# Attention steps: the transposes of the probabilities in turn with projection matmuls on TensorE

## The reference

```python
h = _rms_norm(x, norm_attn_g[l])
proj = h @ w_in[l]
qa, ka, va, fa, qb, kb, vb, ga, gb = jnp.split(proj, split_points, axis=-1)
log_f = jax.nn.log_sigmoid(fa.astype(jnp.float32) + b_forget[l].astype(jnp.float32))
oa = _fox_attention(qa..., ka..., va..., log_f)      # 8 heads of 64, causal, with a forget bias
qb = _partial_rope(qb..., positions)
kb = _partial_rope(kb..., positions)
ob = _dilated_mixture(qb, kb, vb...)                 # 12 heads of 64, windows with dilation 1, 4, 16
ya = oa.reshape(B, S, FOX_W) @ w_branch_a[l]
yb = ob.reshape(B, S, DIL_OUT_W) @ w_branch_b[l]
mixed = jax.nn.sigmoid(ga) * ya + jax.nn.sigmoid(gb) * yb
x = x + mixed @ w_out[l]
h = _rms_norm(x, norm_mlp_g[l])
x = x + jnp.square(jax.nn.relu(h @ w_up[l])) @ w_down[l]
```

## Time and profile before

| what | before |
| --- | --- |
| median of three runs | 1581.77 us |
| lowest and highest run | 1577.9 and 1582.29 us |
| the profiled execution's own time | 1580.75 us |
| its span, first to last instruction | 1578.9 us |
| TensorE matmul busy | 1508.9 us (96%), 7364 instructions |
| VectorE busy | 1094.0 us (69%) |
| ScalarE busy | 797.1 us (50%) |
| mean granted TensorE clock | 0.993 |

### The profile page before, as it was taken

The page is one execution under the profiler, slowest core; times in us unless marked ns, Lnnn a source line. Parts: engine busy times, 40 slices in busy tenths (PEclk is TensorE's granted clock), DMA queues, the critical chain, the costliest instruction groups (busy, mean ns, idle before and its releaser), DMA issues. The chain is left out here.

```text
span 1578.9 us, 20832 instructions
## 1 busy us (share of the span) xinstructions
PE 1508.9 (96%) x7364; PEld 1242.5 (79%) x7364; DVE 1094.0 (69%) x1747; ACT 797.1 (50%) x1438; POOL 9.5 (1%) x24
## 2 busy tenths in 40 slices
PE   6999999998999999999999999999999899999997
PEld 5788887886888888788888878888888677777776
DVE  5687777755756768843665676666666887777776
ACT  5577666653767775534224453343334444444442
POOL 1000000000000000000000000000000000000001
PEclk9999999999999999999999999999999999999999
DMA  5321111111022113333635424444446664444402
GB/s 187 95 67 28 41 54 41 31 38 27 19 63 68 28 41 91 97 107 107 214 120 160 134 86 150 165 151 149 147 147 210 236 226 147 147 147 147 147 27 107
DMA packets 168277, 173.40 MB, mean 110 GB/s; under 512 B 7848, under 2 KB 127720, under 8 KB 167792
## 3 DMA queue, kind: packets, MB, share of 16 engines
q1 hardware_dynamic: 168176, 172.07, 33.9%
HBM read 125.84 MB, written 46.20 MB: 109 GB/s over the span
## 5 line engine op out<-in xcount | busy, mean ns | idle before, releaser
L1131 PE MATMUL ps<-hspl,wsp 128*128 128x512 f32 x1536 | 422.5, 408 | 6.6 <-ACT tmp L1572 3.1
L1131 PEld LDWEIGHTS ps<-hspl,wsp 128*128 128x128 f32 x1536 | 265.0, 189 | 53.1 <-ACT tmp L1572 5.8
L1483 PE MATMUL ps<-dn_b,a_hi 128*128 128x512 f32 x896 | 280.1, 394 | 18.7 <-DVE keep L2328 13.1
L1483 PEld LDWEIGHTS ps<-dn_b,a_hi 128*128 128x128 f32 x896 | 168.2, 190 | 61.1 <-issue 22.9
L1483 PE MATMUL ps<-dn_b,a_lo 128*128 128x512 f32 x448 | 175.8, 392 | 0.0
L2328 DVE TENSOR_TENSOR keep<-keep,ps 128x512 f32<-128x512 f32 (+1 forms) x144 | 101.6, 713 | 41.7 <-PE ps L1483 23.4
L1483 PE MATMUL ps<-up_b,a_hi 128*128 128x512 f32 x384 | 118.5, 390 | 0.6 <-DVE up_b L2328 0.6
L1944 ACT ACTIVATE keep<-keep 128x512 f32<-128x512 f32 x64 | 40.5, 633 | 125.6 <-DVE keep L2630 42.0
L1483 PEld LDWEIGHTS ps<-dn_b,a_lo 128*128 128x128 f32 x448 | 84.8, 189 | 17.9
L2328 DVE TENSOR_TENSOR dn_b<-dn_raw,dn_b 128x1024 fp32r<-128x1024 f32 x56 | 67.1, 1221 | 39.4 <-ACT dn_b L1960 39.4
L2215 DVE TENSOR_TENSOR keep<-ps,o_part 64x256 f32<-64x256 f32 x80 | 39.7, 496 | 76.8 <-ACT o_part L1665 76.3
(11 more groups left out here) (242 smaller groups left out, 2823.9 us busy)
## 6 DMA issues: line engine op xcount, KB each, us to landing
hidden<-keep SPq DMA_DIRECT2D x112, 256.0 KB, 2.2
dn_raw<-hidden SPq DMA_DIRECT2D x56, 512.0 KB, 6.1
raw<-in_w_in SPq DMA_DIRECT2D x35, 512.0 KB, 3.7
a_raw<-in_w_up SPq DMA_DIRECT2D x36, 256.0 KB, 3.1
sgl<-sg SPq DMA_DIRECT2D x8, 1024.0 KB, 5.1
a_raw<-in_w_down SPq DMA_DIRECT2D x32, 256.0 KB, 3.1
spare<-in_w_down SPq DMA_DIRECT2D x32, 256.0 KB, 3.9
spare<-in_w_up SPq DMA_DIRECT2D x28, 256.0 KB, 3.2
```

The lines of the kernel that those rows point to most:

```text
L1131: ins = pe.matmul(psp(u, g), wsp[c % 2][:, wp, k * P:(k + 1) * P], hspl[:, mp, k, cols], start=(n == 0), stop=(n == 23), skip_group_check= ...
L1483: ins = pe.matmul(o, a_part(n, j, wp, k), b_block(n, j, mp, k), start=(first and k == 0 and m == 0), stop=(k == ks - 1 and m == 2), skip_g ...
```

## The change: what it does, and the diff

On TensorE, `project_part` goes, and two helpers take its place. `share(G)` gives what group a step works on, how many matmuls are the step's and which part of the group. `project_next(G, a, b)` issues the step's matmuls from a to b. `transposes` now takes how many of the next step's matmuls are issued already (`ahead`) and whether there is a step to take them from (`more`); behind each transpose it issues one projection matmul while the step has any left, and it gives the new count back. In `mixer_steps` the first third stays ahead of the transposes, and what is left of the step's matmuls after them follows. A step's set of instructions, the waits and the signals are the same.

```diff
-            def project_part(G, part):
+            def share(G):
                 t, s = divmod(G, STEPS)
-                if t < MIX:
-                    for u, g, steps in group_steps(t):
-                        if s in steps:
-                            per = 24 // len(steps)
-                            a = (s - steps[0]) * per
-                            project(u, g, a + per * part // 3, a + per * (part + 1) // 3)
+                return [(u, g, 24 // len(steps), s - steps[0]) for u, g, steps in group_steps(t) if s in steps]
+
+            def project_next(G, a, b):
+
+                for u, g, per, n in share(G):
+                    if a < min(b, per):
+                        project(u, g, n * per + a, n * per + min(b, per))
...
-            def transposes(G):
+            def transposes(G, ahead, more):
+
                 pe.wait_ge(exp_done, G + 1)
...
                     for k in range(a, b):
                         ins = pe.transpose(PS[2][:, (u % 2) * HALF + (k - a) * P:(u % 2) * HALF + (k - a + 1) * P],
                                            probs(G)[:, k * P:(k + 1) * P], ident[:])
-                    ins.then_inc(tr_done, 1)
+                        if k == b - 1:
+                            ins.then_inc(tr_done, 1)
+                        if more:
+                            project_next(G + 1, ahead, ahead + 1)
+                            ahead += 1
+                return ahead
...
+                    ahead = sum(per // 3 for _, _, per, _ in share(G)) if G < last else 0
                     if G < last:
-                        project_part(G, 0)
+                        project_next(G, 0, ahead)
                     if first <= G - 1 < last:
-                        transposes(G - 1)
+                        ahead = transposes(G - 1, ahead, G < last)
                     if G < last:
-                        project_part(G, 1)
-                    if G < last:
-                        project_part(G, 2)
+                        project_next(G, ahead, 24)
```

## The result

The changed kernel takes 1589.74 us (median of seven runs, 1587.31 to 1593.36) against 1582.29 us before in the same comparison. The ratio is 1.0049 with a 95% interval of 1.0035 to 1.0063, so 5.5 to 10.0 us slower. The forecast was 7.3 us more than before and 1588.0 us.

A forecast was written before the change was run, and what follows sets the result against it. The order of TensorE's own work was taken to bound the kernel, busy 218 of 226 us in the attention windows. Terms of 0 + 4.4 + 2.1 + 0.8 = 7.3 us on 1580.75 gave 1588.0 us, range 1580 to 1596.

The forecast's parts named there:

- Term 1: TensorE's new order itself: a transpose alternating with projection matmuls costs the same 0.11 us as in a row, so 0.
- Rival B: Weight loads vanish behind projection matmuls on TensorE, each interleaved transpose 0.05 us shorter: 1576.9 us; chance 0.09.
- Term 2: Even steps of the forgetting pairs: later casts delay ScalarE's exponentials, so the next transposes wait, 4.4 us together.
- with two smaller ones 0.4 us: Last head pair: wait for exponentials of 0.25 us at G = 154 plus two smaller waits, 0.4 us together.
- Everything else on TensorE is fed in time: Attention stretch: of TensorE's listed waits the change touches only the projection matmul's wait for ScalarE's evacuation, 2.0 us.
- Term 3: ScalarE's evacuations come later, so a group's first projection matmul waits: 2.1 us at three long ones, 0.8 at small ones.
- rival A: The waits are swallowed, part caught up later in the kernel: 0 to 4 us left, 1581 to 1585 us; chance 0.22.
- Rival C: ScalarE and VectorE fall behind for good, each of 32 even forgetting steps paying nearly its whole delay: 1600 us; chance 0.15.

The follow-up runs named there:

- e1_dilated: Changed kernel with the old order back in the forgetting pairs, interleaving only in the dilated pairs; attention +0.0 us against before, 1582.49 us in one run.
- e3_even: Changed kernel interleaving only in even steps, old order in odd ones; attention +7.3 us against before without a clock dip, time ratio 1.0037 to 1.0069.
- e2_odd: Changed kernel interleaving only in odd steps, old order in even ones; attention +2.2 us against before, time ratio 1.0008 to 1.0036.
- e6_s2: Changed kernel with the old order back, but more projection matmuls ahead of the transposes in each pair's step 2; 1576.27 us against 1582.41 before.
- e8_even_not8: Changed kernel interleaving only in even steps other than each pair's step 8, old order elsewhere; attention +5.0 us against before, one run.
- e4_two: Changed kernel with two projection matmuls behind each transpose instead of one; attention +17.4 us against before without a clock dip, ratio 1.0084 to 1.0162.

## Why the prediction was right, term by term

**Term 1 (0 us)** held: the dilated pairs are 0.1 us shorter, a pair of transpose and projection matmul takes 0.34 us, and e1_dilated changes nothing. In this kernel a transpose costs 0.109 us in either order. Rival B fell with this. The gap of about 56 ns that the Trainium skill gives an isolated matmul of 128 columns ("TensorE: Matmul & The Clock Gate", "Back-to-back issue gap") counts no weight load and is not met here, where each transpose brings one of its own. Nor are the 81 ns that the same section of the Trainium skill gives such a matmul in a stream of weight loads and matmuls; the 0.109 us measured decide. Why a transpose costs 0.109 us (that the load of the next weights sets it) was argued, not shown.

**Term 2 (4.4 us)**, from one transposes' start to the next, by kinds:

| kind | slack used | forecast | measured, each |
| --- | --- | --- | --- |
| six transposes (G = 108, 124, 140, 156) | 0.42 | 0.27 | 0.28 to 0.29 |
| eight, four behind (110, 126, 142, 158) | 0.49 to 0.55 | 0.33 to 0.39 | 0.34 to 0.35 |
| eight, first step of a pair (112, 128, 144) | 0.83, last 0.38 | 0.5 | 0.51 |
| last pair (150, 152, 154) | 0.38 at 154 | 0.4 in all | 0.13, 0.08, 0.65 |

The sum is 4.9 us. The first three kinds came out within 0.04 us each. The term that was mis-sized is "with two smaller ones 0.4 us": at G = 154 I followed only the exponentials (0.25; e3_even, where VectorE's delay is away, lost 0.14 there from transposes to transposes and 0.26 from scores to scores), where the low parts on VectorE were the later of the two releasers, behind a chain over ScalarE's side work that e2_odd laid open. The 0.08 at G = 152 is within the scatter of that place.

"Everything else on TensorE is fed in time" was not so either. TensorE also waits 3.4 us for the split values and 1.2 us for a group's weights in the forgetting pairs. The change moved neither, so the sum didn't suffer; the wait for the split values is what e6_s2 gained from.

**Term 3 (2.1 + 0.8 us)**: 0.69, 0.71 and 0.70 us at the three long evacuations; 0.27, 0.29 and 0.30 at the small ones instead of 0.2, 0.2 and 0.33, 0.86 in all. e8_even_not8 took the three long ones away, 2.1 of its 2.2 us.

**What the sum left out.** 4.9 + 2.1 + 0.9 = 7.9 us; the forgetting pairs lost 9.0, so the forecast's 7.3 was 1.6 us short of the attention's 8.9. Most of the rest is 0.05 to 0.09 us in each turn that follows a wait. After a wait the first transpose is followed by its projection matmul 0.09 us later (495.86 to 495.95 above), in an unbroken row 0.03 us later (496.26 to 496.29): a released transpose has a price of its own, 0.06 us over some 15 waits. That it is a weight load without cover is likely, not shown.

**The sum and the time.** 8.9 us of attention against 7.3 forecast; 7.45 us between the medians, with 5.5 to 10.0 as their interval. The medians agree with the forecast more closely than its terms deserve. Behind the attention nothing was caught up, which rival A needed: 964.6 and 964.4 us before, 963.0 and 965.1 after, with the clock dips in it. Rival C (VectorE and ScalarE fall behind for good) was true for one step of 32, G = 156.

## What to carry to other kernels

This is what this kernel showed; no other was run. An engine that is nearly always busy can still be one turn of a loop through other engines, and the loop's slack is the work between a producer's last piece and the next thing it needs. Spreading that work between the pieces delays the last piece and removes the cover at the same time; moving the whole block does neither, and here was free but for the evacuations, which stand outside the loop (3.3 us against 8.9). Read such slacks from starts in two engines' timelines, per kind of step, and look at each releaser of the waiting instruction, not only at the one that is last today. Work that can be moved belongs where the engine already waits: that gained 6 to 7 us here.

## What the runs showed of the hardware

- A 128 x 128 float32 transpose costs 0.109 us of TensorE among transposes and among matmuls of 512 columns alike.
- TensorE's granted clock fell from its upper level (2.4 GHz) to the lower (1.2 GHz) for 3.4 us at a time (three times in these runs for 6.8, and for 4.4 to 6.4 at the very end), three to nine times an execution; at the same places in both profiles of the kernel before, at different ones in the two of the changed kernel. While it lasts a matmul of 512 columns takes 0.427 us instead of 0.230, so a dip that falls into dense work costs about 8 x 0.197 = 1.6 us (1.59 in e3_even, 1.58 in e4_two, from their steps' starts against kernels without one). In e3_even one fell into the attention at 531 us, behind the longest wait of that stretch (1.8 us), a wait that the changed kernel had too without a dip. Such dips are as large as the effects studied here, and only profiles tell them apart.
- The attention's 537 us repeat within 0.3 us from profile to profile, and but for one wait that hangs on a transfer each step repeats within 0.04 us, while whole runs of one kernel spread by 0.2 to 0.7%.
